# Keys' and values' products laid into the last linear head, the heads' outputs turned one head later, PSUM 3+2+3 in the sample stage

## The reference

```
h = rmsnorm(x);  P = h @ w_in                    # columns: q, k, v, a, b, z of A; q of B; kv of B (768); gates
q, k, v = silu(causal_conv(P_qkv))               # A, per head of 128
u, w = solve(I + tril(beta * k k^T * decay)), ...  # chunked WY form
for each chunk: v_new = u - w S;  o = q_dec S + (q k^T * decay) v_new;  S = S * last + k_dec^T v_new
o_A = rmsnorm(o, gain) * silu(z)
k_cmp, v_cmp, k_slc, v_slc, k_win, v_win = split(P_kv)   # B: prompt and sample tokens
B: softmax over compressed blocks -> top 16 blocks -> selected + window softmax, for prompt and sample
y = rmsnorm(x + (sigmoid(gA) * (o_A @ Wa) + sigmoid(gB) * (o_B @ Wb)) @ w_out)
```

## Time and profile before

| what | value |
|---|---|
| median of 3 runs | 2217.33 us (2216.51 to 2223.64) |
| profiled execution | 2221.69 us |
| its span | 2219.9 us |
| mean granted TensorE clock | 0.967 of full speed |
| PE busy | 2056.8 us (93%) |
| VectorE busy | 875.0 us (39%) |
| ScalarE busy | 581.8 us (26%) |
| POOL busy | 131.2 us (6%) |
| DMA moved | 151.20 MB |

### The profile page before, as it was taken

The page is one execution under the profiler, slowest core; times in us unless marked ns, Lnnn a source line. Parts: engine busy times, 40 slices in busy tenths (PEclk is TensorE's granted clock), DMA queues, the critical chain, the costliest instruction groups (busy, mean ns, idle before and its releaser), DMA issues. The chain is left out here.

```text
span 2219.9 us, 37574 instructions
## 1 busy us (share of the span) xinstructions
PE 2056.8 (93%) x16009; PEld 1383.3 (62%) x16009; DVE 875.0 (39%) x2213; ACT 581.8 (26%) x1473; POOL 131.2 (6%) x144
## 2 busy tenths in 40 slices
PE   8899999999999997799999999598878999999998
PEld 5566667676766665457777777454666666666543
DVE  3546454564655464102666667244320100100112
ACT  3323232332323232002444445233350000000000
POOL 1001010010101010000000000122220000000000
PEclk9899999998999998899999999799997999999999
DMA  4101011111111010402000000688784111120021
GB/s 137 38 21 40 20 41 31 33 37 30 31 30 49 2 31 18 153 10 70 11 20 10 1 10 1 206 296 297 254 313 152 34 34 33 43 56 0 0 68 60
DMA packets 121583, 151.20 MB, mean 68 GB/s; under 512 B 27865, under 2 KB 105089, under 8 KB 112865
## 3 DMA queue, kind: packets, MB, share of 16 engines
q1 hardware_dynamic: 110724, 76.78, 12.4%
q0 software_dynamic: 10704, 72.16, 9.1%
HBM read 136.83 MB, written 16.26 MB: 69 GB/s over the span
## 5 line engine op out<-in xcount | busy, mean ns | idle before, releaser
L842 PE MATMUL g_ps<-hT,W 128*128 128x352 f32 x1440 | 495.2, 473 | 0.2
L842 PEld LDWEIGHTS g_ps<-hT,W 128*128 128x128 f32 x1440 | 253.7, 192 | 99.1 <-issue 4.8
L2613 DVE SCALAR_TENSOR_TENSOR m_sg<-m_sg,m_ps 128x352 f32<-128x352 f32 x48 | 25.0, 521 | 361.0 <-PE m_ps L2553 361.0
L1626 PE MATMUL p_ps<-hT,Wpair 128*128 128x352 f32 x384 | 130.2, 468 | 1.3 <-DMA Wpair<-in_w_in_dram 0.6
L2565 PE MATMUL m_ps<-m_Wo,m_mixed 128*128 128x512 f32 (+1 forms) x288 | 124.0, 592 | 1.4 <-DVE m_mixed L2616 1.4
L2579 ACT ACTIVATE m_sg<-m_ps 128x352 f32<-128x352 f32 x48 | 22.3, 464 | 387.5 <-PE m_ps L2546 387.5
L2546 PE MATMUL m_ps<-hT,Wgates 128*128 128x352 f32 x384 | 117.7, 465 | 1.6 <-DVEq L2602 1.6
L2546 PE MATMUL m_ps<-hT,m_Wgates 128*128 128x352 f32 x384 | 115.6, 459 | 0.0
L2042 PE MATMUL s_ps<-identity,s_G 128*128 128x128 f32 x512 | 75.9, 291 | 27.3 <-ACT s_XT L2257 18.9
L2546 PEld LDWEIGHTS m_ps<-hT,Wgates 128*128 128x128 f32 x384 | 74.0, 193 | 43.1 <-issue 1.7
L2546 PEld LDWEIGHTS m_ps<-hT,m_Wgates 128*128 128x128 f32 x384 | 73.0, 190 | 40.6
(11 more groups left out here) (415 smaller groups left out, 3345.4 us busy)
## 6 DMA issues: line engine op xcount, KB each, us to landing
W<-in_w_in_dram SPq DMA_DIRECT2D x32, 512.0 KB, 3.8
n_x<-in_x_prompt_dram SPq DMA_DIRECT2D x8, 512.0 KB, 7.7
g_S<-in_state_gdn_dram SPq DMA_DIRECT2D x8, 512.0 KB, 5.4
out_dram<-g_S POOLq DMA_DIRECT2D x8, 512.0 KB, 3.8
Wpair<-in_w_in_dram SPq DMA_DIRECT2D x16, 256.0 KB, 4.0
Wgates<-in_w_in_dram SPq DMA_DIRECT2D x8, 512.0 KB, 5.2
m_Wgates<-in_w_in_dram SPq DMA_DIRECT2D x8, 512.0 KB, 4.7
m_Wo<-in_w_out_dram SPq DMA_DIRECT2D x1, 4096.0 KB, 14.5
```

Of the source, the lines that this page charges most:

```text
L842: ins = pe.matmul(ps[:, k.bank, 0:w], W[:, c_, kt, :], hT[:, kt, t0:t0 + w], start=kt == 0, stop=kt == KT - 1)
L1626: ins = pe.matmul(ps[:, fill_bank(n), 0:w], W[:, "qz".index(x), kt, :], hT[:, kt, t0:t0 + w], start=kt == 0, stop=kt == KT - 1)
```

## The change

Six things change. (1) In the last head, SP fetches the weights of keys and values: the first half into `W` (room of q, k, v), the second into `X3`, once these are free; 8 of the 18 units are laid into the last head's fills: three products in each step of the recursion, two and four at the sample rows, the rest before the outputs. ScalarE copies them out (`keep`). stage_kv makes only the other 10, loads no weights, and turns the position weights behind its second unit. (2) The outputs of head i-1 are turned behind the M products of head i, and VectorE gates z and evicts them there; the last head's stay at its end. (3) In the levels m = 1 to 3 of heads 0 to 6, `fill(1)` behind level_u becomes `fill(2)`. (4) The conv state's rows go through the ring RA and are stored in six pieces. (5) Tiles move: several of stage_gdn's tiles now lie in the rooms of `KV` and `oBT`, the prompt stage's in those of `W` and `X3`, which live longer. (6) In stage_sample the rings get 3, 2 and 3 banks.

The diff, cut to its core:

```diff
+KV_EARLY, KV_AFTER = 8, (2, 5, 7)
...
+        kv_room = g.KV[:].rearrange("p t n -> p (t n)")
+        Y3 = kv_room[:, 0:3 * T].rearrange("p (x t) -> p x t", x=3)
+        T3 = kv_room[:, 3 * T:4 * T]
+        SQ = kv_room[:, 4 * T:6 * T].rearrange("p (x t) -> p x t", x=2)
+        TTp, Tp = (kv_room[:, n:n + TT * Q].rearrange("p (t j) -> p t j", t=TT) for n in (6 * T, 6 * T + TT * Q))
         zh = sb("zh", [P, T])
...
+        kvW = [W[:].rearrange("p a k n -> p (a k n)")[:, 0:KT * 384], X3[:].rearrange("p a n -> p (a n)")[:, 0:KT * 384]]
+        kvW = [w.rearrange("p (k n) -> p k n", k=KT) for w in kvW]
...
+                if i + 1 == HEADS:
+                    cols = w_in[0].rearrange("(k p) n -> p k n", p=P)
+                    sp.wait_ge(proj_filled, RP.at("v2", i).full)
+                    sp.dma_start(kvW[0], cols[:, :, C_KV:C_KV + 384]).then_inc(kvw_loaded[0], 16)
+                    sp.wait_ge(y_half, 3 * HEADS + 3)
+                    sp.dma_start(kvW[1], cols[:, :, C_KV + 384:C_KV + 768]).then_inc(kvw_loaded[1], 16)
+                    for n in range(2):
+                        sp.wait_ge(kvw_loaded[n], 16)
...
+            gp.wait_ge(act_emptied, RA.at("L5", HEADS - 1).done)
+            for n in range(3):
+                part = slice(n * D, (n + 1) * D)
+                gp.dma_start(conv_p[0, 0][:, part], last_rows[n][0:3, :]).then_inc(tail_stored, 16)
+                gp.dma_start(conv_s[0].rearrange("b r n -> (b r) n")[:, part], last_rows[n][3:27, :]).then_inc(tail_stored, 16)
...
+            def keep(n):
+                t, half = divmod(n, 2)
+                k = RP.at(f"kv{n}", HEADS - 1)
+                act.wait_ge(proj_filled, k.full)
+                act.copy(g.KV[:, t, half * 384:half * 384 + 384], ps[:, k.bank, 0:384]).then_inc(proj_emptied, 1)
...
+            def keep(n, kt):
+                t, half = divmod(n, 2)
+                k = RP.at(f"kv{n}", HEADS - 1)
+                if kt == 0:
+                    pe.wait_ge(proj_emptied, k.free)
+                    pe.wait_ge(kvw_loaded[half], 16)
+                ins = pe.matmul(ps[:, k.bank, 0:384], hT[:, kt, t * P:(t + 1) * P], kvW[half][:, kt, :],
+                                start=kt == 0, stop=kt == KT - 1)
+                if kt == KT - 1:
+                    ins.then_inc(proj_filled, 1)
...
+            def outputs(i):
+                pe.wait_ge(o_ready, i + 1)
+                for u, us in enumerate(tiles_of):
+                    k, bank = dve_bank(f"N{u}", i)
+                    pe.wait_ge(dve_emptied, k.free)
+                    for q, t in enumerate(us):
+                        r = rows_of(t)
+                        ins = pe.transpose(bank[:, q * P:q * P + r], Ot[0:r, t, :], c["ident"][0:r, 0:r])
+                    ins.then_inc(dve_filled, 1)
...
+                kv_parts = [(n, kt) for n in range(KV_EARLY) for kt in range(KT)]
+                parts = iter(next_parts + z_parts if more else z_parts + kv_parts)
 
                 def fill(n):
-                    for head, x, s, kt in itertools.islice(parts, n):
-                        project(head, x, s, kt, kt + 1)
+                    for part in itertools.islice(parts, n):
+                        if len(part) == 2:
+                            keep(*part)
+                        else:
+                            project(*part, part[3] + 1)
...
                 products(i, 3)
+                if i:
+                    outputs(i - 1)
                 fill(3)
...
-                        fill(1)
+                        fill(2 if more and m < 4 else 1)
...
-                    fill(2)
+                    fill(2 if more else 1)
...
-                fill(16)
-                pe.wait_ge(o_ready, i + 1)
...
+                fill(len(next_parts + kv_parts))
+                if not more:
+                    outputs(i)
...
+                    z_gated(i - 1)
+                    outputs(i - 1)
...
+        units = [divmod(n, 2) for n in range(KV_EARLY, 2 * TT)]
...
-            for s in range(2):
-                sp.dma_start(W[:, :, s * 384:(s + 1) * 384],
-                             w_in[0].rearrange("(k p) n -> p k n", p=P)[:, :, C_KV + s * 384:C_KV + (s + 1) * 384]
-                             ).then_inc(w_loaded[s], 16)
...
+            for n, (t, s) in enumerate(units):
+                r = P if t < PT else SAMPLE
+                R, emptied, filled = ((RA, act_emptied, act_filled), (RD, dve_emptied, dve_filled))[s]
+                k = R.at(f"{'ab'[s]}{t}")
+                pe.wait_ge(emptied, k.free)
+                for kt in range(KT):
+                    ins = pe.matmul(ps[0:r, k.bank, 0:384], hT[:, kt, t * P:t * P + r], kvW[s][:, kt, :],
+                                    start=kt == 0, stop=kt == KT - 1)
+                ins.then_inc(filled, 1)
+                if n == 1:
+                    k = RD.at("pos")
+                    pe.wait_ge(dve_emptied, k.free)
+                    pe.wait_ge(pos_loaded, 64)
+                    for x in range(2):
+                        ins = pe.transpose(ps[:, k.bank, x * CL:(x + 1) * CL], pos_rows[:, x, :], g.ident[0:CL, 0:CL])
+                    ins.then_inc(dve_filled, 1)
...
+                if n in (3, 5):
+                    v.wait_ge(lin_loaded, 64)
+                    x = (n - 3) // 2
+                    v.tensor_tensor(CW[:, x, :, :], rep(blk[:, x, :], 1, CL), rep(posT[:, x, :], 2, P), ALU.mult
+                                    ).then_inc(cw_ready, 1)
...
-        RX = Ring([0, 1], [x for n in range(SEQS) for x in keys(n)])
-        RA = Ring([2, 3], [f"{x}{i}" for i in range(NB) for x in ("S2", "sc")] + [f"T0{i}" for i in range(NB)])
-        RD = Ring([4, 5, 6, 7], ["blk", "gate", "lq"] + [f"{x}{i}" for i in range(NB) for x in ("pT", "V0", "V1")]
...
+        RX = Ring([0, 1, 2], [x for n in range(SEQS) for x in keys(n)])
+        RA = Ring([3, 4], [f"{x}{i}" for i in range(NB) for x in ("S2", "sc")] + [f"T0{i}" for i in range(NB)])
+        RD = Ring([5, 6, 7], ["blk", "gate", "lq"] + [f"{x}{i}" for i in range(NB) for x in ("pT", "V0", "V1")]
...
+            act += [(f"O{t}", i)] + [(f"L{t}", i) for _ in range(not more and t < 6)]
+        act += [(f"G{u}", i + 1) for u in u3 if more]
...
+        dve += [(f"M{u}", i) for u in (4, 0, 1, 2, 3)] + [(f"N{u}", i - 1) for u in u3 if i] + [(f"Y0{n}", i) for n in g2]
...
+    dve += [(f"N{u}", HEADS - 1) for u in u3]
+    proj += [(f"kv{n}", HEADS - 1) for n in range(KV_EARLY)]
```

More of the change, by code:

```diff
@@ L808, in head_turn @@
                         tails(t)
+                    if not more and t in KV_AFTER:
+                        keep(KV_AFTER.index(t))
                 act.wait_ge(act_emptied, RA.at(f"O{PT - 1}", i).done)
@@ L811, in head_turn @@
                 act.activation(Dm[:], Ot[:], ACT.Square).then_inc(squared, 1)
+                for n in range(len(KV_AFTER), KV_EARLY) if not more else ():
+                    keep(n)
                 if more:
@@ L1163, in step, with z_gated, outputs @@
                     ins.then_inc(v_step, 1)
-                    v.wait_ge(v_step, n_.next())
+                    v.wait_ge(v_step, steps.next())
+                def z_gated(j):
+                    v.wait_ge(z_tanh, j + 1)
+                    step(v.scalar_tensor_tensor(zh[:], zt[:], 1.0, zh[:], ALU.add, ALU.mult))
+                def outputs(j):
+                    for u, us in enumerate(tiles_of):
+                        k, bank = dve_bank(f"N{u}", j)
+                        v.wait_ge(dve_filled, k.full)
+                        w = len(us) * P if u < 2 else SAMPLE
+                        t0 = us[0] * P
+                        v.scalar_tensor_tensor(oAT[:, ds(j, 1), t0:t0 + w].rearrange("p a n -> p (a n)"), bank[:, 0:w],
+                                               gain[:, 0:1], zh[:, t0:t0 + w], ALU.mult, ALU.mult
+                                               ).then_inc(dve_emptied, 1)
+                    v.wait_ge(dve_emptied, RD.at("N2", j).done)
+                    v.sem_inc(o_done, 1)
                 v.wait_ge(coef_ready, i + 1)
@@ L1500, in _ @@
         def _(act):
-            for t in range(TT):
+            for t in (t for t, s in units if s == 0):
                 n = P if t < PT else SAMPLE
@@ L2761, in sb2 @@
                     return second.enter_context(nc.sbuf_tensor(name, shape, F32))
+                g.W = sb2("W", [P, 4, KT, P])
+                g.X3 = sb2("X3", [P, 3, 3 + SEQ + NB * 7])
                 g.KV = sb2("KV", [P, TT, 6 * P])
+                with ExitStack() as first:
+                    parts = const_parts()
+                    width = sum(a.size for a in parts.values()) // P
+                    g.ctile = first.enter_context(nc.sbuf_tensor("consts", [P, width], F32))
+                    g.consts = consts
+                    g.c = Packed(g.ctile, parts)
+                    g.beta = first.enter_context(nc.sbuf_tensor("beta", [P, TT, HEADS], F32))
```

(6 more changed lines are left out.)

142 lines of the change are left out of this document (39 added, 103 removed).

## The result

The changed kernel takes 2140.54 us (median of 4 runs, 2135.68 to 2143.34), the kernel before beside it 2216.92 (4 runs): a ratio of 0.9651, 95% interval 0.9619 to 0.9683, 76 us less. The profiled execution took 2135.68 us with a span of 2133.9; its span is 86.0 us shorter than that of before. 5.6 of these lie ahead of the first M product (95.8 us into the span before, 90.2 now).

A forecast was written before the change was run, and what follows sets the result against it. PE was taken to set the time in the heads, losing it to waits, stalls and half clock. Terms 11.6 + 10 + 13 + 27 + 8.5 = 70.1 us off 2221.7, less 2 for the run shown, gave 2150 us, range 2136 to 2172.

The forecast's parts named there:

- The 13.2 us before M: Seven heads: PE's 1.89 us wait for a bank before the second M group goes; term 11.6 us after VectorE's queue.
- the half of VectorE's 0.46 us a head: First level of seven heads: VectorE comes up to 0.5 us late, 3.2 in all; half of it charged.
- The level products: Levels 1 to 3 of seven heads: three more products fill instruction-fetch stalls; 10 us, bounds 0 and 12.5.
- The clock: Heads: seven stretches at half clock lose 15.2 us; with stalls shortened, 13 us comes back, bounds 0 and 15.2.
- Last head and keys' and values' stage: Early weights and products laid into the last head's waits; ten units left in the stage; 27 us, bounds 24 and 30.
- 30 us of slack cover them: Last head: the two new weight loads land well before the first product needing them, after 853 us.
- Sample stage: A third bank ends PE's waits on ScalarE: 5 us compressed, 3.5 selected; term 8.5 us, bounds 3 and 12.
- clock and fetch stay: Rival, 20%, in the heads: products don't fill the fetch stalls and the clock falls anyway; 2173 us.
- VectorE's queue: Rival, 8%: 2.83 us shows before each head's first level, and the clock still falls five times; 2177 us.
- the sample stage is bound by DMA: Rival, 13%: DMA bounds both the compressed and selected phases, so the 8.5 us term goes; 2158.5 us.
- Late weights: Rival, 3%: weights come late in the last head, so products don't hide; one load time more, 2159 us.
- Slower rooms for VectorE's tiles: Rival, 2%: VectorE's instructions take longer on tiles in shared rooms; decides only beyond factor 1.75, 2390 us at 2.3.

The follow-up runs named there:

- e3: Changed kernel with one product behind each level_u in all heads, as before, and three more at the head's end: 2149.40 us, ratio to before 0.9714.
- e2: Changed kernel with every head's outputs turned at that head's own end again: 2153.50 us, ratio to before 0.9725.
- e5: Changed kernel with outputs at each head's own end and one product behind each level_u, both undone at once: 2170.24 us, ratio to before 0.9786.
- e7: Changed kernel with three products in place of two behind level_u in levels 1 to 3 of the seven heads: 2150.85 us, ratio to before 0.9722.
- e1: Changed kernel with the sample stage's rings as before, 2, 2 and 4 banks: 2153.40 us, ratio to before 0.9733.
- e10: Changed kernel with the second half of the keys' and values' weights fetched only after the last head's 64-blocks: 2137.89 us, ratio to before 0.9658.

## Why the prediction held, and where it did not

The time lay 9 us below the 2150 us forecast, inside the range; the sum of terms was 70.1 us, the medians differ by 76.4, and the pieces of the two profiled executions by 78.3. (The upper ends of the bounds add 12.8 us to the sum, not the 14 from which the range was made.)

**The heads, forecast 34.6 us; measured 36.5** (37.7 less the 1.2 that now count to the last head). The 13.2 us before M went whole; the half of VectorE's 0.46 us a head that I charged did not show: between the first level products and the next ones that need VectorE's result PE turns v and makes two products of the fill, and no wait on VectorE is in the trace. The level products gave 9.4 us, forecast 10: "issue" in L907 and L896 was 15.7 us and is 8.8, but 4.3 of that belong to the last head (1.8 before); the seven others went from 13.9 to 4.5. e3 alone shows less of it, 6.5. The clock gave 15.2 of 15.2, forecast 13: no stretch at half clock lies between 110 and 780 us. The reason given for it is not borne out. I took five of the seven stretches for the M wait's and two for the level stalls', as if each wait brought its own. With the M wait alone back, three of its seven come with half clock (e2); with both back there are five stretches, of which two follow an M wait (e5). How the two kinds of stall share the 15.2 us stays open, since single executions with the same heads already differ by a stretch.
The Trainium skill ("Runtime: NRT & Kernel Launch", section "Instruction fetch mechanics") would have the crossing of an instruction block mostly hidden; here it is not on runs of 0.19 us products. In the seven heads the stalls take 11.0 us with one product behind level_u (e3), 4.5 with two and 0.4 with three (e7), and each ends 2.2 to 2.9 us after a 16 KB packet's start.

**Last head and keys' and values' stage, forecast 27; measured 25.2** (24.0 and the 1.2), bounds 24 to 30. Steps of 3.49 us (forecast 3.47), no wait before the outputs, a first unit 1.49 us after them (3.5 to 4.2 forecast, 1.3 for the evictions and 2.2 to 2.9 for the block change), and the ten units ended at 928.1 (near 933 forecast). What I did not see is a cost put at nothing: "30 us of slack cover them" was true for the two loads, but not for what shared the DMA with them. The 3 MB in the level loop held up the fetch of the program: the last head's "issue" went from 1.8 to 4.3 us, and 1.7 went to half clock. That the term came out near 27 is in part luck: these 4.2 us and the 2.0 to 2.7 gained ahead of the first unit, neither of them forecast, partly cancel.

**Sample stage, forecast 8.5, bounds 3 to 12; measured 16.6** (15.6 by e1). The forecast was about half of what the term gave, and its bounds didn't hold it. The step that failed: "in the selected phase the DMA share is already 0.96 at 362 GB/s ... so only what is not DMA's can go". The selected part, from its first scores to the merge, went from 124.1 to 114.2 us, 9.9 where 3.5 was forecast; the compressed part, from its first scores on, from 131.4 to 125.7, 5.7 where 5 was; the remaining 1.0 lies ahead of the first scores. A busy share near 1 was read as a bound. But three steps in a row ran at 393 to 402 GB/s, 9 to 11% more, with a share of 0.99 to 1.02 in place of 0.96: the share does not say how much is left.
The Trainium skill ("DMA: Bandwidth & Descriptors", section "Bandwidth") gives about 358 GB/s as what binds traffic between HBM and SBUF, and in the same section has 425 GB/s for one core that loads alone. These three steps of one core ran 10 to 12% above the first figure, which is no limit here; the measurement decides.

**The rivals.** That clock and fetch stay did not come: no stretch at half clock is left in the seven heads, and 4.5 of their 13.9 us of "issue". VectorE's queue did not come either: no wait on it is in the trace. That the sample stage is bound by DMA is refuted by e1. Late weights: no wait on them. Slower rooms for VectorE's tiles: its M evictions take 332 ns on average, 331 before, its taps 1278 and 1278.

Open stays why e10's short stalls grow as the long one goes (0.95 us less "issue" in all, and 1.7 of clock, give 2.65 of which *last* shows 2.1); and by what the packet stands behind the load.

## To carry to other kernels

A DMA share near 1 in a loop does not by itself show a bound (0.96 at 362 GB/s became 0.99 at 393): look whether the loop's own chain has a wait that another bank would end, and try it. Short waits of a busy TensorE can cost twice, once as they stand and once in the clock after them; five of seven waits of 1.89 us were followed by half clock before, three of seven in e2. Since that differs from execution to execution, judge such edits by several of them. Before a large load is moved into "free" DMA time, see what else uses the DMA there: here the program's own packets did, and PE stood still where it came to its next instructions before they had landed.

## What was not expected of the hardware

The 16 KB instruction packet in the last head started at 786.1 us, just when 3 MB at 372 GB/s had passed, and took 1.1 us; PE had stopped at 785.7 and went on at 788.5. With the second half of the load out of the way the stall at the same products was 0.82 us (e10); with both loads in place and PE later at them there was none (e2). In all 13 traces each of those 154 level stalls ended 2.2 to 2.9 us after such a packet's start. One core's gathers held 393 to 402 GB/s over three steps of 11.9 us.
